# Decoder layer with 32 experts on one core: the experts' gather reads normalised rows, router, conversion and fill order rewritten

## The chip, the cores and the metric

One Trainium2 chip, one core of it. The metric is the device time of one launch in microseconds (us); of the kernel before three timed runs and one profiled execution are shown.

## What is computed

One inference step of one decoder layer (width 1024) for 256 prompt tokens and 8 sample tokens that share all weights:

```
y    = x @ w_in -> short convolution and dilated attention (12 heads)
x    = LN1(alpha * x + mixed @ w_out)
x    = LN2(alpha * x + memory_attention(x))          4 heads over 256 memory rows
g    = softmax of the 4 largest of (x @ w_router + b_router), 32 experts
y_e  = swiglu(x_e @ w_gate_up[e] + b_gate_up[e]) @ w_down[e] + b_down[e]
x    = LN3(alpha * x + sum over the chosen experts of g_e * y_e)
```

An expert's weights are 12 MB in float32 (8 MB gate and up, 4 MB down), 384 MB for all 32; everything else that is read is below 100 MB.

## The kernel before

Everything is written by hand as one stream of instructions for each engine, with semaphores between them. SP issues nearly all loads. A table of loads (`STREAM`) runs through a ring of 12 slots of 1 MB; a slot is loaded again when `reader_done` says that its reader is through.

**Projection and heads.** TensorE multiplies x by w_in in split float32 (`win_half`, L1641); after the second half `small_turns` (L1580 to L1588) makes the bias table and turns the small parameters (convolution weights, gains and shifts of the two norms) into columns; VectorE copies them out (L1015 to L1019) before it goes on with the low parts of w_in (L991). Then comes a pipeline over steps 0 to 13 for the 12 attention heads. In step s TensorE does `scores(s)` (L1689, L1690), `probs_turned(s - 1)` (transposes, L1697) and `values(s - 2)` (L1706 to L1708); VectorE does `head_max(s)`, in the steps `KEYS_AT = (1, 2, 4, 5, 6, 7, 8, 10)` also the key products and sums of one sample sequence (L1096, L1088), and then `head_norm(s)` (L1135), for which `probs_turned(s)` of the next step waits. In step 0 VectorE does the samples' own scores between the two. The table `FILL` puts 8 half products of the memory keys and values (`dense_half`, 8 matmuls of 128x512 each, L1608) behind the work of certain steps: `{1: 0, 2: 1, 4: 2, 5: 3, 7: 4, 8: 5, 10: 6, 11: 7}`.

**Second norm.** The output product of memory attention is the last `dense_half("wmo", 3)`, four tiles, between which TensorE does single small products of the samples' norm (`sample_means` L1809, `sample_squares` L1814); VectorE adds each tile to the residual (L1212) and computes the samples' norm (L1276 to L1292). `layer_norm(1)`: x is kept as columns (`xT`); TensorE turns it to rows in PSUM (L1822), VectorE takes the statistics, ScalarE writes the normalised rows `xh` (L892), TensorE turns them back (L1829, L1836), and ScalarE and VectorE apply gain and shift chunk by chunk (L896, L1249).

**Router.** Logits of all tokens in one product with w_router as the stationary side (L1935), bias (L1388), transposes of the logits (L1948), and of the finished x back to rows (L1942); VectorE finds the 4 largest (L1398 to L1413), TensorE counts (L1960, L1963), VectorE makes positions and the 0/1 matrix `Sel` (L1445), and ScalarE, VectorE and GpSimd cut the rows of x into three bfloat16 parts `x3` (L937, L1421, L941, L775; samples L1472, L1473). Then `gather` multiplies the parts with `Sel` (L1972, samples L1974), ScalarE copies the result to `xTe` (L952 or L962), VectorE makes the gates (L1477 to L1480), `SelG` (L1455), scales x by alpha (L1484) and copies the turned gates (L1488), and releases TensorE's expert loop.

**Experts.** Loop over 16 pairs of experts: `gate_up` (L2001) of both with the scatter of the pair before between its chunks (L2050), `down` (L2034), the turned activations (L2021), the next `gather`. 16 slots of 1 MB hold the experts' weights; SP fills them in units of two (L626, L622) as TensorE is done with each. After the last pair `sum_turned` (L2071) puts x as rows into PSUM, L2110 adds the last scattered results, and `last_layer_norm` (L1221, L1301, L1307) ends the kernel.

## Time and profile before

| what | value |
|---|---|
| median of 3 timed runs | 1330.09 us (1328.61 to 1330.22) |
| the profiled execution | 1329.79 us, its span 1328.0 us |
| TensorE busy, weight loads | 1228.7 us (93%), 580.6 us |
| VectorE, ScalarE, GpSimd busy | 375.4, 202.5, 39.0 us |
| moved by DMA | 485.08 MB, mean 365 GB/s |
| GB/s, slices 13 to 39 of 40 | 401, then 425 to 432 |
| GB/s, slice 12 | 135 |
| mean granted TensorE clock | 0.981 |

A slice is 33.2 us. Busy shares of engines are means over stages with different limits; a trace row gives the start, how long the group took, the engine, the line, what it writes and reads with shapes, how many records it has (a float32 matmul leaves two, a transpose or a bfloat16 matmul one), and in brackets how long the engine sat idle before it and what ended that.

### The profile page before, as it was taken

The page shows a single profiled execution, that of the slowest core. Times are in us where ns is not written, and L with a number is a line of the kernel's source. Part 1 is how long each engine was busy: PE and PEld are TensorE (multiplying, and loading weights), DVE is VectorE, ACT ScalarE, POOL GpSimd, SP SyncE. Part 2 cuts the span into 40 slices and gives each one's busy share as a digit, 9 for nine tenths or more (in the row PEclk, how much of TensorE's full clock was granted, in tenths as well). Part 3 has the DMA queues.
Part 4 walks back from the last instruction along what each step waited for, and adds up shares of the span by engine and source line. Part 5 has one row for each costly group of instructions (what it writes and reads, how often), then busy time and mean ns, then how long its engine had stood idle before and what let it go on. Part 6 is the DMA issues. An engine that isn't in the chain of part 4 may idle for free.

```text
span 1328.0 us, 16323 instructions
## 1 busy us (share of the span) xinstructions
PE 1228.7 (93%) x6536; PEld 580.6 (44%) x6536; DVE 375.4 (28%) x921; ACT 202.5 (15%) x334; POOL 39.0 (3%) x62
## 2 busy tenths in 40 slices
PE   7998999989879999999999998989899898989986
PEld 6994446675643343433433233333333233333323
DVE  3645532471353022121221302122020202212123
ACT  4443131122120110100101010010101011010001
POOL 2201000000010000000000000000000000000001
PEclk8998899999879999999999999999999999999998
DMA  9984767388939999999999999999999999999993
GB/s 324 246 273 164 215 214 268 107 328 331 365 135 401 426 426 428 426 430 427 427 427 427 428 428 429 426 427 428 427 426 432 426 426 427 427 427 427 428 425 128
DMA packets 62628, 485.08 MB, mean 365 GB/s; under 512 B 6176, under 2 KB 6516, under 8 KB 34336
## 3 DMA queue, kind: packets, MB, share of 16 engines
q1 hardware_dynamic: 58720, 469.46, 87.0%
q0 software_dynamic: 3872, 15.12, 3.5%
q8 instruction: 25, 0.41, 0.1%
q14 instruction: 11, 0.09, 0.0%
HBM read 479.40 MB, written 5.17 MB: 365 GB/s over the span
## 4 chain that ended last, share of the span: by engine, by line
PE 60%; DMA 33%; DVE 4%; ACT 1%; SPq 1%; issue 1%; DVEq 0%; ACTq 0%
PE ps L2001 25%; DMA ring<-in_w_gate_up_dram 15%; DMA late<-in_w_gate_up_dram 13%; PE ps L1608 10%; PE ps L1641 5%; PE ps L2050 5%; PE ps L2034 5%; DMA ring<-in_w_down_dram 3%; DMA ring<-in_cache_mem_v_dram 1%; PE ps L1972 1%; PE ps L1775 1%; PE ps L2058 1%; DVE arena L1221 1%; DMA ring<-in_w_in_dram 1%; PE ps L1793 1%
## 5 line engine op out<-in xcount | busy, mean ns | idle before, releaser
L2001 PE MATMUL ps<-ring,arena 128*64 128x512 f32 x1536 | 359.8, 600 | 14.9 <-DMA ring<-in_w_gate_up_dram 14.9
L1510 DVE TENSOR_TENSOR arena<-arena,ps 128x264 f32<-128x264 f32 x128 | 55.2, 431 | 574.5 <-PE ps L2050 574.5
L2001 PEld LDWEIGHTS ps<-ring,arena 128*64 128x64 f32 x1536 | 99.0, 136 | 201.3 <-issue 160.7
L2034 PE MATMUL ps<-ring,arena 128*64 128x512 f32 x768 | 171.3, 596 | 14.9 <-DMA ring<-in_w_down_dram 14.9
L2034 PEld LDWEIGHTS ps<-ring,arena 128*64 128x64 f32 x768 | 53.8, 137 | 119.7 <-issue 105.8
L957 ACT ACTIVATE arena<-arena 128x512 f32<-128x512 f32 x32 | 20.2, 632 | 471.2 <-DVE arena L1493 471.2
L2050 PE MATMUL ps<-arena 128*128 128x264 f32 x256 | 91.2, 438 | 0.0
L2001 PE MATMUL ps<-late,arena 128*64 128x512 f32 x384 | 90.0, 596 | 0.0
L1608 PE MATMUL ps<-arena,ring 128*128 128x256 f32 x384 | 87.0, 381 | 1.4 <-ACT arena L896 0.7
L2050 PEld LDWEIGHTS ps<-arena 128*128 128x128 f32 x256 | 38.1, 188 | 103.8 <-issue 103.8
L1641 PE MATMUL ps<-x_split,w_split 128*128 128x264 f32 x384 | 74.5, 295 | 7.3 <-DVE arena L1001 5.1
L1608 PEld LDWEIGHTS ps<-arena,ring 128*128 128x128 f32 x384 | 71.1, 189 | 14.4 <-issue 3.1
L1641 PEld LDWEIGHTS ps<-x_split,w_split 128*128 128x128 f32 x384 | 62.4, 197 | 7.9 <-DVE x_split L997 5.1
L1972 PE MATMUL ps<-arena 128*128 128x128 bf16 x768 | 54.9, 223 | 8.2 <-DVE arena L1473 8.2
L1608 PE MATMUL ps<-ring,arena 128*128 128x512 f32 x128 | 61.0, 632 | 0.0
L1641 PE MATMUL ps<-x_split,ring_split 128*128 128x264 f32 x192 | 56.2, 293 | 0.0
L1972 PEld LDWEIGHTS ps<-arena 128*128 128x128 bf16 x768 | 51.9, 100 | 8.4 <-issue 8.3
L2001 PE MATMUL ps<-arena 96*64 96x512 bf16 (+1 forms) x256 | 50.7, 495 | 4.0 <-DMA late<-in_w_gate_up_dram 3.1
L1493 DVE TENSOR_SCALAR arena<-ps 128x512 f32<-128x512 f32 x32 | 22.2, 693 | 109.9 <-PE ps L2001 109.4
L959 ACT COPY arena<-ps 128x512 f32<-128x512 f32 x32 | 18.8, 587 | 219.7 <-PE ps L2021 219.7
L2034 PE MATMUL ps<-late,arena 128*64 128x512 f32 x192 | 44.2, 595 | 6.2 <-DMA late<-in_w_down_dram 6.2
L2001 PEld LDWEIGHTS ps<-late,arena 128*64 128x64 f32 x384 | 25.8, 136 | 45.2 <-issue 42.2
(301 smaller groups left out, 983.2 us busy)
## 6 DMA issues: line engine op xcount, KB each, us to landing
ring<-in_w_gate_up_dram SPq DMA_DIRECT2D x96, 2048.0 KB, 33.8
ring<-in_w_down_dram SPq DMA_DIRECT2D x48, 2048.0 KB, 34.3
late<-in_w_gate_up_dram SPq DMA_DIRECT2D x16, 2048.0 KB, 33.8
arena<-in_w_gate_up_dram SPq DMA_DIRECT2D x16, 1024.0 KB, 31.5
late<-in_w_gate_up_dram SPq DMA_DIRECT2D x16, 1024.0 KB, 34.2
late<-in_w_down_dram SPq DMA_DIRECT2D x8, 2048.0 KB, 35.3
ring<-in_w_in_dram SPq DMA_DIRECT2D x12, 1024.0 KB, 16.9
ring<-in_cache_mem_k_dram SPq DMA_DIRECT2D x8, 1024.0 KB, 6.1
```

The source lines that it names most:

```text
L957: nc.scalar.activation(sg_, g2, ACT.Sigmoid, scale=1.702).then_inc(e_sig, 1)
L959: nc.scalar.copy(actT, ps[:, 2, :].rearrange("p (q n) -> p q n", q=4)).then_inc(e_at_out, 1)
L1221: nc.vector.bn_stats(stats[0:n, t, 6 * j:6 * j + 6], ps[0:n, bank + j, :]).then_inc(dve_own, 1)
L1493: nc.vector.tensor_scalar(g2, ps[:, b, :], 7.0, None, ALU.min).then_inc(e_g2, 1)
L1510: nc.vector.tensor_tensor(xT[:, c, :], xT[:, c, :], ps[:, 2 + c % 2, 0:T], ALU.add).then_inc(e_y_out, 1)
L1608: ins = mm(out(n), lhs(w, k, kk), rhs(w, k, kk), start=(kk == 0), stop=(kk == 7))
L1641: ins = mm(ps[:, n % 4, 0:T], w[:, cols], x[kk], start=(kk == 0 and m == 0), stop=(kk == 7 and m == 2))
L1775: ins = mm(out, w, v, start=(t == 0), stop=(t == terms[-1]))
L1972: mm(out, x3[:, t, k, P * c:P * c + P], Sel[:, t].rearrange("p a s -> p (a s)"), start=(t == 0 and k == 0), stop=False)
L2001: ins = mm(ps[64 * j:64 * j + 64, 6 * a + gu, :], x, w[:, D * gu + 512 * j:D * gu + 512 * j + 512], start=(c < 0), stop=(c == 7), skip_gro ...
L2034: ins = mm(ps[64 * j:64 * j + 64, 4 + half, :], x, w[:, kk, 512 * half:512 * half + 512], start=(m == 0), stop=(m == 7), skip_group_check= ...
L2050: mm(ps[:, 2 + c % 2, 0:T], yb[:, half, P * (c % 4):P * (c % 4) + P], SelT[:, half, :], start=True, stop=True).then_inc(e_y, 1)
```

## The change

1. `FILL` becomes `{0: 0, 1: 1, 3: 2, 5: 3, 7: 4, 8: 5, 10: 6, 11: 7}`; `KEYS_AT` stays.
2. `small_turns` also turns gain and shift of the second norm into columns in the order in which the gather delivers channels (8 more matmuls), with one more copy on VectorE.
3. The three bfloat16 parts are cut from the normalised rows `xh2`, before gain and shift: rows 0 to 127 by four instructions on GpSimd, rows 128 to 255 by three conversions on ScalarE, between which TensorE subtracts with `minus` (minus the identity) in PSUM. Gain and shift are applied behind the gather: channels 0 to 3 by four instructions on ScalarE, 4 to 7 by four on VectorE, with a semaphore each, and TensorE waits for the second only at chunk 4.
4. The samples' rows are taken as float32, turned in `sample_rows` inside `dense_half("wmo", 3)` behind its third tile (`sample_squares` moves up one tile), and gathered by a float32 matmul over 8 rows instead of a bfloat16 one over 72.
5. Logits are made per chunk with x as the stationary side (`logits_of`), between the transposes of the second norm, so that they come out as rows; those of the samples earlier (`sample_logits`, with 6 matmuls that only keep TensorE at work).
6. Memsets go from VectorE to GpSimd, before the norm. On VectorE the gates now stand behind `x_scaled(2)`.
7. In the last pair `sum_turned` stands inside `gate_up` and `down`, and the last norm's statistics wait for each half of a tile.

```diff
-FILL = {1: 0, 2: 1, 4: 2, 5: 3, 7: 4, 8: 5, 10: 6, 11: 7}
+FILL = {0: 0, 1: 1, 3: 2, 5: 3, 7: 4, 8: 5, 10: 6, 11: 7}
...
+            for tl in (lgt, posm):
+                nc.gpsimd.memset(tl, 0.0).then_inc(s_low, 1)
+            pool.wait_ge(s_sc, H + MH)
+            nc.gpsimd.memset(yb, 0.0).then_inc(s_yz, 1)
+            pool.wait_ge(s_yz, 1)
+            pool.dma_start(yb[0:NX], b_down[0].rearrange("e (h n) -> e h n", h=2)).then_inc(s_first, 16)
             pool.wait_ge(s_dn, 56)
             pool.dma_start(g3[:, 0, :], ln3_g.broadcast_to((P, D))).then_inc(s_g3, 16)
             pool.dma_start(g3[:, 1, :], ln3_b.broadcast_to((P, D))).then_inc(s_g3, 16)
-            pool.wait_ge(s_yz, 1)
-            pool.dma_start(yb[0:NX], b_down[0].rearrange("e (h n) -> e h n", h=2)).then_inc(s_first, 16)
-            for t in range(2):
-                pool.wait_ge(s_x2b, t + 1)
-                nc.gpsimd.tensor_tensor(x3[:, t, 2, :], rest[:, t, :], x3[:, t, 1, :], ALU.subtract).then_inc(s_x3, 1)
+            nc.gpsimd.memset(SelT, 0.0).then_inc(s_yz, 1)
+            hi0 = by_unit(x3[:, 0, 0, :])
+            pool.wait_ge(s_xh, 3)
+            nc.gpsimd.tensor_copy(hi0, every_second(xh2[:, 0, :])).then_inc(s_split, 1)
+            pool.wait_ge(s_split, 1)
+            nc.gpsimd.tensor_tensor(by_unit(rest), every_second(xh2[:, 0, :]), hi0, ALU.subtract).then_inc(s_split, 1)
+            pool.wait_ge(s_split, 2)
+            nc.gpsimd.tensor_copy(x3[:, 0, 1, :], rest).then_inc(s_split, 1)
+            pool.wait_ge(s_split, 3)
+            nc.gpsimd.tensor_tensor(x3[:, 0, 2, :], rest, x3[:, 0, 1, :], ALU.subtract).then_inc(s_split, 1)
...
+                if k == 1:
+                    act.wait_ge(s_srow, 1)
+                    act.wait_ge(s_xz, 1)
+                    nc.scalar.copy(by_unit(xs_rows[0:NS, :]), every_second(psf[0:NS, 3072:3072 + D])).then_inc(
+                        s_srow_out, 1)
+                rows_of = (xh, xh2)[k]
...
-            for t, (_, n) in enumerate(TCH):
-                act.wait_ge(s_x2, t + 1)
-                b = (4, 6, 2)[t]
-                if t == 0:
-                    act.wait_ge(s_xz, 1)
-                nc.scalar.copy(by_unit(x3[:, t, 0, :] if t < 2 else xs3[0:n, :]),
-                               every_second(psf[0:n, 512 * b:512 * b + D])).then_inc(s_x1, 1)
-            for t, (_, n) in enumerate(TCH):
-                act.wait_ge(s_xr, t + 1)
-                nc.scalar.copy(x3[:, t, 1, :] if t < 2 else mid_s[0:n, :],
-                               rest[:, t, :] if t < 2 else rest_s[0:n, :]).then_inc(s_x2b, 1)
-            act.wait_ge(s_rt_out, 3)
+            rest1 = psf[:, 512 * ROWB[1]:512 * ROWB[1] + D]
+            nc.scalar.copy(by_unit(x3[:, 1, 0, :]), every_second(xh2[:, 1, :])).then_inc(s_three, 1)
+            act.wait_ge(s_less, 1)
+            nc.scalar.copy(x3[:, 1, 1, :], rest1).then_inc(s_three, 1)
+            act.wait_ge(s_less, 2)
+            nc.scalar.copy(x3[:, 1, 2, :], rest1).then_inc(s_three, 1)
+            act.wait_ge(s_route, 2)
             nc.scalar.activation(rex, rex, ACT.Exp).then_inc(s_gex, 1)
+            def x_scaled(n):
+                act.wait_ge(e_gx, n)
+                for c in range(4):
+                    ins = nc.scalar.activation(xTe[:, c, :], ps[:, 6, P * c:P * c + P], ACT.Identity,
+                                               bias=gather_gb[:, 1, c:c + 1], scale=gather_gb[:, 0, c:c + 1])
+                ins.then_inc(e_gx_out, 1)
...
-                dve.wait_ge(s_ln, 2 * k + i + 1)
+                if k < 2:
+                    dve.wait_ge(s_ln, 2 * k + i + 1)
                 for j in range(2):
+                    if k == 2:
+                        dve.wait_ge(s_ln, 4 + 2 * i + j + 1)
...
+                if k == 1:
+                    dve.wait_ge(s_low, 5)
+                    dve.wait_ge(s_rts, 1)
+                    link(nc.vector.tensor_tensor(lgt[0:NS, 2, :], ps[0:NS, 7, 2 * NX:3 * NX], brow[0:NS, :], ALU.add))
+                    link(nc.vector.max(top8[:, 2, :], lgt[:, 2, :]))
...
-                link(nc.vector.tensor_tensor(x_s, x_s, tokens(sums_s[:, 0, :]), ALU.mult))
-                link(nc.vector.tensor_tensor(x_s, x_s, channels(gcol[k]), ALU.mult))
+                nc.vector.tensor_tensor(squares_s, x_s, tokens(sums_s[:, 0, :]), ALU.mult).then_inc(s_xhs, 1)
+                dve.wait_ge(s_xhs, k + 1)
+                link(nc.vector.tensor_tensor(x_s, squares_s, channels(gcol[k]), ALU.mult))
...
-            dve.wait_ge(s_kvst, 96)
-            for tl in (lgt, posm, gat, SelT, yb):
-                ins = nc.vector.memset(tl, 0.0)
-                if tl is not yb:
-                    own[0] += 1
-                    ins.then_inc(dve_own, 1)
-            ins.then_inc(s_yz, 1)
-            dve.wait_ge(dve_own, own[0])
             dve.wait_ge(s_rt, 1)
-            nc.vector.tensor_scalar(lgTs[0:NX, :], ps[0:NX, 0, 0:T], brc[0:NX, :], None, ALU.add).then_inc(
-                s_rt_out, 1)
-            dve.wait_ge(s_rt, 2)
-            own[0] += 2
-            nc.vector.tensor_copy(lgt[:, 0:2, :], ps[:, 1, 0:2 * NX].rearrange("p (t e) -> p t e", t=2)).then_inc(
-                dve_own, 1)
-            nc.vector.tensor_copy(lgt[0:NS, 2, :], ps[0:NS, 1, 2 * NX:3 * NX]).then_inc(dve_own, 1)
-            dve.wait_ge(dve_own, own[0])
-            for t in range(3):
+            link(nc.vector.tensor_tensor(lgt[:, 0:2, :], ps[:, 6, 0:2 * NX].rearrange("p (t e) -> p t e", t=2),
+                                         brow.unsqueeze(1).broadcast_to((P, 2, NX)), ALU.add))
+            for t in range(2):
...
+            def x_scaled(n):
+                dve.wait_ge(e_gx, n)
+                for c in range(4, DC):
+                    ins = nc.vector.tensor_scalar(xTe[:, c, :], ps[:, 7, P * (c - 4):P * (c - 4) + P],
+                                                  gather_gb[:, 0, c:c + 1], gather_gb[:, 1, c:c + 1], ALU.mult,
+                                                  ALU.add)
+                ins.then_inc(e_gx_odd, 1)
             select(0)
...
+            x_scaled(2)
...
+                every = par_rows[0:n_par, :].rearrange("p (q s) -> p s q", s=2)
+                for i in range(2):
+                    row = 6 + DC * (2 + i)
+                    to = ps[:, 6, 96 + DC * i:96 + DC * i + DC].rearrange("p (u s) -> p s u", s=2)
+                    for j in range(2):
+                        of_row = ident[0:n_par, row:row + DC].rearrange("p (u j) -> p j u", j=2)[:, j, :]
+                        for s in range(2):
+                            ins = mm(to[64 * j:64 * j + 64, s, :], every[:, s, :], of_row, start=True, stop=True)
+                ins.then_inc(s_bt, 1)
...
+            def sample_rows():
+                pe.wait_ge(s_xhs, 2)
+                for c in range(DC):
+                    ins = tp(psf[0:NS, 3072 + P * c:3072 + P * c + P], squares_s[:, c, :], ident)
+                ins.then_inc(s_srow, 1)
+            def sample_logits():
+                pe.wait_ge(s_xs, 2)
+                pe.wait_ge(s_srow_out, 1)
+                pe.wait_ge(s_late, 16)
+                for c in range(DC):
+                    ins = mm(ps[0:NS, 7, 2 * NX:3 * NX], x_s[:, c, :], wr[:, c, :], start=(c == 0), stop=(c == DC - 1),
+                             skip_group_check=True)
+                ins.then_inc(s_rts, 1)
+                stay_awake(6, ps[:, 6, 0:P])
+            def logits_of(c):
+                for t in range(2):
+                    ins = mm(ps[:, 6, NX * t:NX * t + NX], xT[:, c, P * t:P * t + P], wr[:, c, :], start=(c == 0 and t == 0),
+                             stop=(c == DC - 1), skip_group_check=True)
+                return ins
...
+                    if k == 1:
+                        logits_of(c - 4)
+                for c in range(4, DC):
+                    pe.wait_ge(s_lt_odd if c % 2 else s_lt_out, 4 * k + c // 2 + 1)
+                    if k == 1:
+                        ins = logits_of(c)
+                if k == 1:
+                    ins.then_inc(s_rt, 1)
...
-            dense_half("wmo", 3, out_columns, {0: lambda: sample_means(1), 2: lambda: sample_squares(1)})
-            layer_norm(1)
-            pe.wait_ge(s_xs, 2)
-            pe.wait_ge(s_late, 16)
-            for c in range(DC):
-                ins = mm(ps[0:NX, 0, 0:T], wr[:, c, :], xT[:, c, :], start=(c == 0), stop=(c == 7))
-            ins.then_inc(s_rt, 1)
-            def x2_rows(t):
-                (t0, n), b = TCH[t], (4, 6, 2)[t]
-                for c in range(DC):
-                    ins = tp(psf[0:n, 512 * b + P * c:512 * b + P * c + P], xT[:, c, t0:t0 + n], ident)
-                ins.then_inc(s_x2, 1)
-            x2_rows(0)
-            pe.wait_ge(s_rt_out, 1)
-            for t, (t0, n) in enumerate(TCH):
-                ins = tp(ps[0:n, 1, NX * t:NX * t + NX], lgTs[0:NX, t0:t0 + n], ident[0:NX, 0:NX])
-            ins.then_inc(s_rt, 1)
-            x2_rows(1)
-            x2_rows(2)
-            stay_awake(8, ps[:, 0, 384:512])
-            pe.wait_ge(s_rt_out, 2)
-            pe.wait_ge(s_low, 2)
+            dense_half("wmo", 3, out_columns, {0: lambda: sample_means(1), 1: lambda: sample_squares(1),
+                                               2: sample_rows})
+            layer_norm(1, sample_logits)
...
+            rest1 = [ps[:, ROWB[1] + j, :] for j in range(2)]
+            pe.wait_ge(s_low, 5)
+            for j in range(2):
+                rows = every_second(xh2[:, 1, :])[:, 2 * j:2 * j + 2]
+                mm(rest1[j], ident, rows, start=True, stop=False, skip_group_check=True)
+            pe.wait_ge(s_three, 1)
+            for j in range(2):
+                ins = mm(rest1[j], minus, x3[:, 1, 0, 512 * j:512 * j + 512], start=False, stop=True,
+                         skip_group_check=True)
+            ins.then_inc(s_less, 1)
...
-                    ins = mm(out, xs3[0:64 + NS, P * c:P * c + P], Sel[0:64 + NS, 2].rearrange("p a s -> p (a s)"),
+                    ins = mm(out, xs_rows[0:NS, P * c:P * c + P], SelS[0:NS].rearrange("p a s -> p (a s)"),
                              start=False, stop=True)
-                ins.then_inc(e_gx, 1)
-            pe.wait_ge(s_xr, 3)
-            pe.wait_ge(s_x3, 4)
+                    if c % 4 == 3:
+                        ins.then_inc(e_gx, 1)
...
+                    if last and a == 1 and c == 3:
+                        pe.wait_ge(e_st_out, 3 * it + 4)
+                        sum_turned(1, 1)
+                        pe.wait_ge(e_u2, 2 * it + 2)
+                        sum_turned(2, 0)
+                    if last and a == 1 and c == 4:
+                        sum_turned(2, 1)
...
-                if last:
-                    pe.wait_ge(e_st_out, 3 * it + 4)
-                    for t, half in ((2, 0), (2, 1), (1, 1), (0, 0), (0, 1)):
-                        sum_turned(t, half)
-                else:
+                if not last:
```

TensorE in the attention steps 0 to 2. Before (L1689 and L1690 are scores, L1697 the transposes, L1608 a fill):

```order
L1689 MATMUL ps<-arena 128x128
L1690 MATMUL ps<-arena 128x256
L1689 MATMUL ps<-arena 128x128
L1690 MATMUL ps<-arena 128x256
L1697 MATMUL ps<-arena,late 128x128 x3
L1608 MATMUL ps<-ring,arena 128x512 x8
L1689 MATMUL ps<-arena 128x128
L1690 MATMUL ps<-arena 128x256
L1697 MATMUL ps<-arena,late 128x128 x3
```

and with the change (the same instructions are L1721, L1722, L1729 and L1640):

```order
L1721 MATMUL ps<-arena 128x128
L1722 MATMUL ps<-arena 128x256
L1640 MATMUL ps<-ring,arena 128x512 x8
L1721 MATMUL ps<-arena 128x128
L1722 MATMUL ps<-arena 128x256
L1729 MATMUL ps<-arena,late 128x128 x3
L1640 MATMUL ps<-ring,arena 128x512 x8
L1721 MATMUL ps<-arena 128x128
L1722 MATMUL ps<-arena 128x256
L1729 MATMUL ps<-arena,late 128x128 x3
```

The first fill stands ahead of the first transposes, and step 2 no longer has one.

TensorE from the last half product (L1640) to the first transposes of the second norm (L1879), with the change (L1841 means, L1846 squares, L1852 `sample_rows`, L1861 `sample_logits`):

```order
L1640 MATMUL ps<-arena,ring 128x256 x4
L1841 MATMUL ps<-arena 128x8
L1640 MATMUL ps<-arena,ring 128x256 x4
L1846 MATMUL ps<-arena 128x8
L1640 MATMUL ps<-arena,ring 128x256 x4
L1852 MATMUL ps<-arena 8x128 x8
L1640 MATMUL ps<-arena,ring 128x256 x4
L1879 MATMUL ps<-arena 128x128 x16
L1861 MATMUL ps<-arena 8x32 x8
```

Before, tiles 2 and 3 were one row of x8, the squares (L1814) stood behind them, and nothing stood for L1852 and L1861.

VectorE from the selection to the last copy before the expert loop, with the change (L1452 and L1454 `Sel`, L1475 `x_scaled(2)`, L1491 to L1494 the gates, L1464 to L1468 `advance`, L1497 alpha, L1502 the turned gates):

```order
L1454 TENSOR_TENSOR arena<-arena,late 128x256
L1458 CAST arena<-arena 96x128
...
L1486 TENSOR_SCALAR nswi<-late 1x1 x4
L1475 TENSOR_SCALAR arena<-ps,arena 128x128 x4
L1491 TENSOR_TENSOR late<-late 128x96
...
L1494 TENSOR_TENSOR late<-late 128x96
...
L1497 TENSOR_SCALAR arena<-arena 128x2112
L1502 COPY arena<-ps 32x264 x2
```

Before, nothing of L1475 stood there, and two instructions for the samples' parts (L1472, L1473) stood in its place.

## Rows read from the trace of the kernel before

**Rows 1.** Chain that ended last, start us, us, what

```profile
306.14 16.86 DMA ring<-in_cache_mem_v_dram
...
410.72 2.27 PE ps L2001 x12
...
464.62 2.27 PE ps L2001 x12
...
1220.99 34.60 DMA ring<-in_w_gate_up_dram
```

**Rows 2.** Windows: busy us of PE, PEld, DVE, ACT, POOL; PEclk; DMA share; GB/s

```profile
384.00:386.00 2.00, 1.94 (x19) 1.97 (x20) 1.86 (x7) 0.00 (x0) 0.00 (x0) 0.50 0.00 0
```

**Rows 3.** Timeline of TensorE, projection: the small turns and what follows

```profile
30.45 0.61 PE L1582 MATMUL ps<-arena 33*128 33x12 f32 x4
...
33.83 0.39 PE L1641 MATMUL ps<-x_split,w_split 128*128 128x264 f32 x1 [2.19 <-DVE ring_split L991]
```

**Rows 4.** Timeline of TensorE in the attention steps

```profile
108.00 0.90 PE L1697 MATMUL ps<-arena,late 128*128 128x128 f32 x3 [3.39 <-DVE late L1135]
...
119.77 7.13 PE L1608 MATMUL ps<-ring,arena 128*128 128x512 f32 x16
...
130.50 0.55 PE L1697 MATMUL ps<-arena,late 128*128 128x128 f32 x3 [0.62 <-DVE late L1135]
...
154.01 0.90 PE L1697 MATMUL ps<-arena,late 128*128 128x128 f32 x3 [2.93 <-DVE late L1135]
...
156.31 9.18 PE L1608 MATMUL ps<-ring,arena 128*128 128x512 f32 x16
```

**Rows 5.** Timeline, last half product before the second norm

```profile
351.63 1.97 PE L1608 MATMUL ps<-arena,ring 128*128 128x256 f32 x8
...
352.70 0.23 DVE L1290 TENSOR_TENSOR arena<-arena 128x64 f32<-128x64 f32 x1
...
354.12 1.97 PE L1822 MATMUL ps<-arena 128*128 128x128 f32 x16 [0.52 <-DVE arena L1212]
```

**Rows 6.** Timeline from the norm to the first expert's release

```profile
361.99 1.97 PE L1836 MATMUL ps<-arena 128*128 128x128 f32 x8
...
372.03 0.38 DVE L1398 MAX8 late<-late 128x8 f32<-128x32 f32 x3
...
374.16 0.26 DVE L1413 TENSOR_TENSOR late<-late 128x96 bf16<-128x96 f32 x1
...
383.99 0.26 DVE L1477 TENSOR_TENSOR late<-late 128x96 f32<-128x96 f32 x1
...
384.06 0.80 PE L1972 MATMUL ps<-arena 128*128 128x128 bf16 x6 [8.19 <-DVE arena L1473]
...
385.62 1.25 DVE L1484 TENSOR_SCALAR arena<-arena 128x2112 f32<-128x2112 f32 x1
...
390.13 0.76 DVE L1488 COPY arena<-ps 32x264 f32<-32x264 f32 x2 [3.26 <-PE ps L1984]
...
390.96 0.62 PE L2001 MATMUL ps<-arena 96*64 96x512 bf16 x4 [0.86 <-ACT arena L952]
...
395.05 0.33 SPq L626 DMA_DIRECT2D late<-in_w_down_dram  x1
```

**Rows 7.** Timeline of VectorE and GpSimd side by side

```profile
379.67 1.92 DVE L1465 TENSOR_SCALAR late<-arena,late 1x4 f32<-1x4 f32 x1
...
379.58 2.00 POOL L775 TENSOR_TENSOR arena<-arena 128x1024 bf16<-128x1024 f32 x1 [0.44 <-ACT arena L941]
```

**Rows 8.** Timeline, the end of the kernel

```profile
1294.85 3.65 PE L2034 MATMUL ps<-ring,arena 128*64 128x512 f32 x16 [1.16 <-DMA ring<-in_w_down_dram]
...
1299.11 5.68 PE L2071 MATMUL ps<-arena 128*8 128x128 f32 x48
...
1304.73 7.09 PE L2034 MATMUL ps<-ring,arena 128*64 128x512 f32 x32
...
1314.76 1.30 DVE L1221 BATCH_NORM_STATS2 arena<-ps 128x6 f32<-128x512 f32 x2 [2.21 <-PE ps L2110]
```

194 lines of the change are left out of this document (105 added, 89 removed).

## The prediction

> **What bounds the kernel now.** I read the chain that ended last first, then windows, then the timeline around each edit. Up to the expert loop the chain is mostly TensorE's own matmuls. It leaves them once for long: memory values that SP issued at 306.14 land at 323.0 [rows 1]. That issue came when VectorE had freed the ring, and VectorE followed TensorE, so the wait moves along with whatever stands ahead of it. I let every us of the prologue count.
>
> In the loop the first two pairs follow each other at 464.62 - 410.72 = 53.9 us [rows 1], TensorE's pace while slots are full. Later the chain is nothing but DMA: 24 loads of 1 MiB (25.17 MB together) at the 427 GB/s of the profile's slices take 58.9 us a pair. The 5 us between make the loop DMA's. Its end is therefore the time at which SP's first issue follows a released slot, 395.05 [rows 6], plus a constant; before that issue the queue lies dry (0 GB/s in 384 to 386, [rows 2]). So **three things count: TensorE's time up to 395.05, nothing inside the loop, and what follows the last landing** [rows 8].
>
> The sum is made against the profiled execution, 1329.79 us, which is 0.3 under the median of the runs; I take them as one. A measurement of this kernel tells about 0.2% (2.7 us) from no change.
>
> **Small turns.** Eight float32 matmuls more, two records each; four records of twelve columns take 0.61 us at first [rows 3], and I take 0.12 us a record: 8 x 2 x 0.12 = 1.9 us. TensorE waits for VectorE already there, 2.19 us [rows 3], and VectorE's copies wait for the turns, so the added time lengthens that wait, and a fifth copy of 0.15 us comes on top. If some lies beside the start of a load it is less: **+1.7**, between 0 and +2.1.
>
> **Fill order.** In steps without a fill TensorE waits for `head_norm`. Before, these waits are 3.39 us (step 0, VectorE also at the samples' scores), 0.62 (step 3, no key products), 2.93 (step 6, key products), and 0.62 again in step 9, which I take from step 3's row: 7.6 us [rows 4]. Now step 0 has a fill of 7.13 us, longer than its wait, and that wait goes. Steps 2, 4, 6 and 9 have none; the first three hold key products, so each should wait 2.93, and step 9 0.62: 9.4 us. Net +1.9. What the old 3.39 hid was VectorE's first step; the 7.13 us cover it.
> Then the clock. Behind each of the two long waits the transposes take 0.90 us instead of 0.55 and the fill 9.18 instead of 7.13 [rows 4], so one fall costs 0.35 + 2.05 = 2.4 us. Behind three such waits it is three falls against two: +2.4. Steps 2 and 4 follow each other closely, so one may fall less than the next: with two falls the part is +1.9, with none 1.9 - 4.8 = -2.9. I take three, since both long waits of before fell and neither short one did: **+4.3**, between -2.9 and +4.3, with +2 more if what follows a fall is longer than the fill.
>
> **Sample rows in the last half product.** TensorE now wants the samples' normalised values behind tile 2, which ends where tile 3's row begins, 351.63. The squares come one tile earlier, but on VectorE the variance still stands behind tile 2's residual (the order of the part on the change), so the values are ready where L1290 ends, 352.93 [rows 5]. TensorE, which ran through, idles 1.3 us with the signal's way, some 1.4, then turns eight chunks, half of L1822's 16 in 1.97 us: 1.0 [rows 5]. **+2.4** before the norm, between +1.0 (values in time) and +3.
>
> **Second norm and router,** counted from T0, the norm's first transpose (354.12). Before, they reach the first `gate_up` at T0 + 36.8 and the gather at T0 + 29.9 [rows 6]; between them stand logits for all tokens, three turns to rows and three rounds of conversion. Now, step by step: turning back ends at T0 + 9.8 [rows 6] plus about 1.2 for the logits put between, plus 0.7 for the last two chunks' gain and shift, plus the last logits: T0 + 12.7. VectorE adds the bias (0.3) and takes two maxima (0.3), then the unchanged chain from the maxima's end to L1413's, 374.42 - 372.41 = 2.0: T0 + 15.4. Counts on TensorE 1.3, the second subtraction 0.5, ScalarE's third conversion of 1024 columns some 1.0 (VectorE's L1484 needs 1.25 for 2112, [rows 6]): T0 + 18. GpSimd starts at T0 + 5 and needs four instructions of 2.0 us each [rows 7], T0 + 13, so it has 5 us in hand. Gather: with the clock full it is half of before's 5.7 us, 3.3 with waits, plus 1.4 for a float32 sample product of two records in place of one in 8 chunks; at half clock it takes 0.5 to 3 more. T0 + 22.7. Then, in VectorE's row, four scalings of 128 columns, 0.35 each between L1290's 0.23 for 64 [rows 5] and L1488's 0.38 for 264 (1.4), gates and `advance` 385.62 - 383.99 = 1.6, alpha 1.25, copies 0.76 [rows 6]: T0 + 27.7, **9.1 us earlier** than 36.8. Here an old cover is gone: before, gates and alpha stood beside a gather of 5.7 us; now TensorE idles some 5 us ahead of `gate_up`. In this profile an idle stretch of 8.19 us [rows 6] left the granted clock at 0.50 [rows 2]. `gate_up` to the release is 4.1 us [rows 6] at full clock; I take +2.4 for the half one, as in the fill, +1.0 for VectorE instructions held up by GpSimd's and +0.5 for the gather. **-5.2**, between -9 and -2.
>
> That VectorE can be held up by GpSimd shows once in the trace: L1465, one partition of four elements, takes 1.92 us and ends with GpSimd's L775 [rows 7]. The Trainium skill's "SBUF — State Buffer", Who interferes with whom, says that a VectorE instruction with two SBUF inputs, or in a two-port mode, and a GpSimd one that reads SBUF shut each other out for the whole instruction. The row agrees; the rule speaks against part 3 of the change, and is behind the second rival.
>
> **Samples and scaling in the loop.** The 1.4 us of float32 sample products make TensorE's pace 55.3 us a pair, still 3.6 under DMA's 58.9; ScalarE's four scalings and VectorE's four stand beside matmuls. Nothing. If DMA did not bind, 14 pairs of 1.4 would be 20 us.
>
> **The end.** The last expert's `down` needs the last two units of 2 MiB. Before, the sums (5.68 us) stand right ahead of it. A unit lands every 4.9 us (2.1 MB at 427 GB/s), and TensorE needs 3.65 us for it [rows 8]. The last then lands near 1294.85 + 2 x 4.9 = 1304.65, and its product ends at 1308.3, where `down` of before ends at 1304.73 + 7.09 = 1311.8 because the sums stood ahead. Only one sum of 0.95 stays behind. -3.1, and the last norm's statistics start on half a tile, which takes about half of 1.30 off: -0.6. **-3.7**, between -4.5 and -1.
>
> **Sum:** 1.7 + 4.3 + 2.4 - 5.2 - 3.7 = -0.5 us: 1329.3.
>
> **Rivals.**
> **1, faster: the clock holds.** TensorE does transposes and values between the waits of steps 2 and 4, and both old falls stood behind something special (step 0 and step 6 with long gaps since the last fill). For it: the 0.62 waits cost nothing. With one fall at most in the heads (-2.9 + 2.4 = -0.5 in place of +4.3) the time is 1324.5; with `gate_up` at full clock too, -2.4 more, 1322.1. Against: a wait of 2.93 fell once already. I take 1325. Chance 0.32.
> **2, slower: GpSimd's conversions come late.** They read every second element, which no row shows on GpSimd, and stand against VectorE's two-input instructions of norm and router. Up to T0 + 18 this is free. From there each us counts. If the two strided ones take twice 2.0, the chain ends at T0 + 5 + 12 = T0 + 17; two or three instructions of VectorE's chain held for 1.9 each [rows 7] then push the selection, hence counts and TensorE's second subtraction, to about T0 + 22: +4, and the gather at half clock another 1.5. 1329.3 + 5.5 = 1334.8. By the rule of that page of the Trainium skill this is what would happen wherever a router instruction meets one of GpSimd's; the row bears it out for one. Chance 0.24.
> **3, the end gains nothing or the loop turns TensorE's.** The sums may stand where TensorE has no pause, and DMA's 58.9 may hide the rest: 3.5 us less gained, 1332.8. Chance 0.08, of which half counts as slower.
> My forecast keeps 0.36.
>
> **Chances.** Faster by over 0.2% (under 1327.4): rival 1 and a little of the forecast's lower side, 0.38. Within: 0.37. Slower (over 1332.7): rival 2 and parts of the forecast and rival 3, 0.25. The likeliest case's own range is 1327 to 1332.5. The range for 8 in 10 must take in both rivals: from 1321.5 (rival 1 whole) to 1336 (rival 2 and a further us of its locks).
>
> **What would show it.** Small turns: the wait ahead of the products that follow them 4 us, not 2.2. Fill: three waits of 2.9 in steps 2, 4, 6, each with transposes of 0.90 behind, none in step 0. Sample rows: TensorE idle 1.6 us ahead of them, released by VectorE. Router: gather starts at T0 + 18, released by ScalarE and not by GpSimd; `gate_up` at T0 + 27.7; PEclk 0.50 there. GpSimd: four instructions of 2 us; VectorE ones stretched to about 2 beside them. End: no sums between the last `down`s, last landing minus first release unchanged. I am wrong if the loop's pace per pair is not 58.9, if the landings move by other than the first release, or if the gather waits for GpSimd.

## The result, and the profile after

The changed kernel is slower: 1344.49 us median of four runs (1343.38 to 1345.7) against 1330.15, ratio 1.0113 with a 95% interval of 1.010 to 1.0125. I had forecast 1329.3 and a range up to 1336. Its profiled execution took 1343.38 us, its span 1341.6.

| us | before | after | difference | forecast |
|---|---|---|---|---|
| first transpose of the second norm (T0) | 354.12 | 363.12 | +9.0 | +8.4 |
| T0 to the gather's start | 29.94 | 24.06 | -5.9 | -11.9 |
| gather's start to first `gate_up` | 6.90 | 15.92 | +9.0 | +2.8 |
| first `gate_up` to SP's first issue | 4.09 | 6.65 | +2.6 | +2.4 |
| that issue to the end of the span | 932.95 | 931.85 | -1.1 | -3.7 |

(The forecast also held 1.5 us for locks and a half-clock gather in rows two and three together.) Up to T0 the forecast stands. From T0 to the release it was 10.9 us off (+5.7 where I had -5.2), and 2.6 more at the end.

From the page of the changed kernel: the clock and GB/s of 40 slices, the shares of the chain that ended last, and groups of instructions (busy us, mean ns, idle before).

```profile
PEclk8999799999959999999999999999999999999999
...
GB/s 324 246 267 176 192 201 264 114 299 367 307 163 285 427 426 427 427 428 427 426 428 427 429 427 428 427 427 428 425 429 428 427 427 427 427 425 429 427 426 147
...
PE 91%; DVE 4%; DMA 2%; ACT 1%; SPq 1%; issue 1%; DVEq 0%; ACTq 0%
...
L2031 PE MATMUL ps<-arena 128*128 128x128 bf16 x768 | 67.5, 225 | 1.1 <-ACT arena L959 1.1
...
L2033 PE MATMUL ps<-arena 8*128 8x128 f32 x256 | 64.2, 331 | 0.0
...
L2062 PE MATMUL ps<-ring,arena 128*64 128x512 f32 x1536 | 358.7, 600 | 0.0
```

Slice 12 has a clock of five tenths, and the chain is 91% TensorE where it was a third DMA. TensorE waits for nothing before its expert products now (0.0 us idle in 1536 records): the loop is no longer DMA's. The 256 records of the samples' float32 product take 331 ns each, half as long again as the 225 ns of a bfloat16 record.

**Attention steps,** timeline of TensorE in the changed kernel, steps 2 to 6:

```profile
126.69 0.55 PE L1729 MATMUL ps<-arena,late 128*128 128x128 f32 x3 [2.93 <-DVE late L1158]
...
127.96 8.83 PE L1640 MATMUL ps<-ring,arena 128*128 128x512 f32 x16
...
142.70 0.90 PE L1729 MATMUL ps<-arena,late 128*128 128x128 f32 x3 [2.93 <-DVE late L1158]
...
159.94 0.90 PE L1729 MATMUL ps<-arena,late 128*128 128x128 f32 x3 [2.93 <-DVE late L1158]
```

Three waits of 2.93 us as forecast. Behind the second and the third the transposes take 0.90 us at once; behind the first the clock fell only within the fill that follows (8.83 us instead of 7.13). Cf. [rows 4].

**From the half product to the first release,** all engines in the changed kernel:

```profile
359.83 1.04 PE L1852 MATMUL ps<-arena 128*8 128x128 f32 x8 [1.33 <-DVE arena L1321]
...
363.12 1.97 PE L1879 MATMUL ps<-arena 128*128 128x128 f32 x16 [0.52 <-DVE arena L1235]
...
368.40 0.86 DVE L1260 SCALAR_TENSOR_TENSOR arena<-arena 128x1 f32<-128x1 f32 x1
...
370.56 1.00 PE L1886 MATMUL ps<-arena 128*128 128x128 f32 x4 [1.77 <-ACT arena L914]
...
375.57 4.32 PE L1869 MATMUL ps<-arena 128*128 128x32 f32 x20
...
379.70 3.76 PE L2000 MATMUL ps<-arena 128*128 128x512 f32 x4
...
382.22 0.26 DVE L1433 TENSOR_TENSOR late<-late 128x96 bf16<-128x96 f32 x1
...
385.42 0.11 PEld L2021 LDWEIGHTS ps<-arena,late 128*128 128x128 bf16 x2 [0.65 <-ACT arena L957]
...
387.18 0.50 PE L2031 MATMUL ps<-arena 128*128 128x128 bf16 x6 [1.15 <-ACT arena L959]
...
397.78 0.50 PEld L2033 LDWEIGHTS ps<-arena 8*128 8x128 f32 x2 [0.20 <-issue]
...
398.61 1.37 DVE L1475 TENSOR_SCALAR arena<-ps,arena 128x128 f32<-128x128 f32 x4 [11.65 <-PE ps L2033]
...
403.10 1.06 PE L2062 MATMUL ps<-arena 96*64 96x512 bf16 x4 [1.39 <-DVEq L1529]
...
409.75 0.33 SPq L633 DMA_DIRECT2D late<-in_w_down_dram  x1
```

Windows of the same stretch (busy us of PE, PEld, DVE, ACT, POOL; PEclk; DMA share; GB/s):

```profile
374.00:376.00 2.00, 2.00 (x12) 2.00 (x11) 0.20 (x2) 1.35 (x2) 0.65 (x1) 0.50 1.08 461
...
386.00:388.00 2.00, 0.85 (x9) 0.71 (x8) 0.85 (x8) 1.92 (x2) 0.00 (x0) 0.95 0.01 4
...
390.00:392.00 2.00, 2.00 (x14) 1.38 (x12) 0.00 (x0) 0.00 (x0) 0.00 (x0) 0.50 0.00 0
...
404.00:406.00 2.00, 2.00 (x8) 0.66 (x6) 0.00 (x0) 0.00 (x0) 0.00 (x0) 0.50 0.00 0
```

To be seen here: the sample rows wait 1.33 us, as I had it. VectorE's L1260 takes 0.86 us beside GpSimd's first instruction (0.16 for the other tile), and TensorE idles 1.77 us between the halves of the turn back. Behind that the clock falls: it is 0.50 from about 370.7 to 384.4, through the logits and the product with the identity (L2000, 3.76 us), then full, and 0.50 again from about 387.8 to 408.3, through nearly the whole gather (387.18 to 398.57) and the first `gate_up`. The counts stand behind L2000 in TensorE's row, though VectorE has the selection at 382.48.

The kernel before had half clock in this stretch too. A window of its norm:

```profile
362.00:364.00 2.00, 1.96 (x8) 1.56 (x8) 1.13 (x4) 1.39 (x3) 0.00 (x0) 0.50 0.96 363
```

Its clock was 0.50 from about 358.4 to 368.7, and from about 378.9 to 389.2 ahead of and in its gather: 20.5 us together between T0 and the release, against 34.1 in the changed kernel. Half clock was not new there; there is more of it now, and more of it lies under work that everything waits for.

**A later pair's gather.** Timeline of TensorE in the changed kernel:

```profile
736.78 0.50 PE L2031 MATMUL ps<-arena 128*128 128x128 bf16 x6
...
737.22 0.48 PE L2033 MATMUL ps<-arena 8*128 8x128 f32 x2
...
737.63 0.51 PE L2031 MATMUL ps<-arena 128*128 128x128 bf16 x6
```

and in the kernel before:

```profile
710.26 0.50 PE L1972 MATMUL ps<-arena 128*128 128x128 bf16 x6
...
710.60 0.22 PE L1974 MATMUL ps<-arena 72*128 72x128 bf16 x1
...
710.66 0.50 PE L1972 MATMUL ps<-arena 128*128 128x128 bf16 x6
```

At full clock a chunk starts 0.85 us after the one ahead of it, and 0.40 before. Eight chunks make 3.6 us a pair: the pairs follow each other at 488.20 - 430.71 = 57.5 us instead of 53.9 [rows 1].

**The end.** Timeline of TensorE in the changed kernel, and below it two windows:

```profile
1310.90 1.86 PEld L2141 LDWEIGHTS ps<-arena 128*128 128x128 f32 x16 [0.81 <-issue]
...
1312.88 0.20 PEld L2102 LDWEIGHTS ps<-ring,arena 128*64 128x64 f32 x4
...
1318.98 0.20 PEld L2102 LDWEIGHTS ps<-ring,arena 128*64 128x64 f32 x4
```

```profile
1316.00:1318.00 2.00, 1.32 (x9) 0.67 (x5) 0.00 (x0) 0.59 (x1) 0.00 (x0) 1.00 0.48 205
...
1318.00:1320.00 2.00, 2.00 (x14) 1.31 (x16) 0.00 (x0) 0.00 (x0) 0.00 (x0) 1.00 0.04 16
```

The last landing is near 1317, but the last `down` runs until 1326.07, 9 us behind it. Before, a like window (1302 to 1304) had 123 GB/s, so the last landing was near 1302.6, and `down` ended at 1311.8, 9.2 us behind; but then 5.68 us of sums stood right ahead of it [rows 8]. From the first release to the last landing it was 907.5 us before and 907.2 now: the landings moved with the release, as I had said, and DMA kept its rate. What is new is that TensorE itself is late. The sums do stand ahead of the last `down`, but TensorE has no wait for DMA left for them to fill.

### The profile page after: what moved, and what is told of

Same layout as the page of the kernel before. It is cut to its first block, busy times and chain, and to the rows that moved or that the text cites. A ratio compares the mean times of both kernels' runs of the same rounds, so it can differ in the third digit from the quotient of the medians.

```text
span 1341.6 us, 16810 instructions
## 1 busy us (share of the span) xinstructions
PE 1290.4 (96%) x6697; PEld 620.7 (46%) x6697; DVE 389.8 (29%) x1002; ACT 208.2 (16%) x380; POOL 43.1 (3%) x68
## 4 chain that ended last, share of the span: by engine, by line
PE 91%; DVE 4%; DMA 2%; ACT 1%; SPq 1%; issue 1%; DVEq 0%; ACTq 0%
PE ps L2062 36%; PE ps L2102 17%; PE ps L1640 10%; PE ps L2120 6%; PE ps L1673 5%; PE ps L2031 4%; PE ps L2033 4%; PE ps L2089 2%; DMA ring<-in_cache_mem_v_dram 1%; PE ps L1807 1%; PE ps L2128 1%; DMA ring<-in_w_in_dram 1%; PE ps L1825 1%; DVE arena L1247 1%; PE ps L1869 0%
## 5 line engine op out<-in xcount | busy, mean ns | idle before, releaser
L2062 PE MATMUL ps<-late,arena 128*64 128x512 f32 x384 | 92.1, 608 | 0.0
L1640 PE MATMUL ps<-arena,ring 128*128 128x256 f32 x384 | 87.1, 381 | 1.6 <-DVE arena L1280 0.9
L1640 PEld LDWEIGHTS ps<-arena,ring 128*128 128x128 f32 x384 | 71.0, 189 | 14.6 <-issue 3.1
L1475 DVE TENSOR_SCALAR arena<-ps,arena 128x128 f32<-128x128 f32 x64 | 21.9, 405 | 184.8 <-PE ps L2033 184.8
L2031 PE MATMUL ps<-arena 128*128 128x128 bf16 x768 | 67.5, 225 | 1.1 <-ACT arena L959 1.1
L2033 PE MATMUL ps<-arena 8*128 8x128 f32 x256 | 64.2, 331 | 0.0
L1640 PE MATMUL ps<-ring,arena 128*128 128x512 f32 x128 | 62.4, 644 | 0.0
L2031 PEld LDWEIGHTS ps<-arena 128*128 128x128 bf16 x768 | 46.6, 100 | 16.1 <-issue 3.2
```

Of the source, the lines that this page charges most:

```text
L1475: ins = nc.vector.tensor_scalar(xTe[:, c, :], ps[:, 7, P * (c - 4):P * (c - 4) + P], gather_gb[:, 0, c:c + 1], gather_gb[:, 1, c:c + 1], A ...
L1640: ins = mm(out(n), lhs(w, k, kk), rhs(w, k, kk), start=(kk == 0), stop=(kk == 7))
L2031: mm(out, x3[:, t, k, P * c:P * c + P], Sel[:, t].rearrange("p a s -> p (a s)"), start=(t == 0 and k == 0), stop=False)
L2033: ins = mm(out, xs_rows[0:NS, P * c:P * c + P], SelS[0:NS].rearrange("p a s -> p (a s)"), start=False, stop=True)
L2062: ins = mm(ps[64 * j:64 * j + 64, 6 * a + gu, :], x, w[:, D * gu + 512 * j:D * gu + 512 * j + 512], start=(c < 0), stop=(c == 7), skip_gro ...
```

## Experiments

Each kernel was timed beside the kernel before on the same chip (its median 1329.7 to 1329.9 in the three sets). "Release" is SP's first issue for a slot that the expert loop freed; it was 395.05 before and is 409.75 in the changed kernel.

**1. Fill order alone, undone in the changed kernel and done in the old one.**

```diff
-FILL = {0: 0, 1: 1, 3: 2, 5: 3, 7: 4, 8: 5, 10: 6, 11: 7}
+FILL = {1: 0, 2: 1, 4: 2, 5: 3, 7: 4, 8: 5, 10: 6, 11: 7}
```

> The changed kernel with the fill order of before. TensorE reaches the second norm at 363.12 us in the changed kernel and at 354.12 before; 4.75 us of these 9.0 arise in the attention steps, and about 1 more in the memory attention, where a wait of 1.95 us left the clock at half. Theory 'fill order' expects the norm's first transpose about 4.8 to 5.8 us earlier (357.3 to 358.3), and as TensorE never waits in the expert loop of the changed kernel, the whole of it at the end: 1338.7 to 1339.7. A rival, 'the memory values' transfer covers it' (TensorE waits until 329.6 for them anyway), expects less than 3 us.

> The kernel before with the new fill order alone. Theory 'fill order': three waits of 2.93 us and three clock falls in the attention steps in place of 3.39, 0.62, 2.93 and two falls cost 4.75 us there, as in the changed kernel; the loop of this kernel is DMA's, so its end follows the first release: 1334.5 to 1335.5, against 1329.7 to 1330.1. The rival (the memory values' transfer hides part of it) expects 1331.5 to 1333.

Measured: 1339.14 us (1336.95 to 1339.89) with it undone, 5.4 less; T0 at 358.12. Done alone in the old kernel: 1334.13 (ratio 1.0029, 1.0018 to 1.0041), 4.3 more; T0 at 358.97, 4.85 later. The order of the fills costs 5.4 us in one kernel and 4.3 in the other (0.4 under the range I had given there), so little of it is covered by anything.

**2. GpSimd later.**

```diff
-            pool.wait_ge(s_xh, 3)
+            pool.wait_ge(s_xh, 4)
```

> The changed kernel, but GpSimd starts its four conversions only when both tiles of normalised rows are written (a wait for 4 in place of 3). In the changed kernel VectorE's L1260 takes 0.86 us beside GpSimd's first conversion (0.16 without), TensorE then idles 1.77 us between the two halves of the turn back, and its clock is at half from about 370.7 to 384. Theory 'lock' expects L1260 at 0.16 us, an idle time of about 1.05 as before, a clock that stays full in the norm as it does before, and so logits 3 to 4 us earlier and the gather about 3 us earlier: 1341 to 1342. Theory 'the clock falls anyway' (the chunks' turns and logits are too thin for it) expects 0.7 us only: 1343.8. GpSimd ends at about T0 + 14, under the gather's T0 + 24, in both.

VectorE's scaling, the halves of the turn back and the last logits in that kernel:

```profile
369.13 0.16 DVE L1260 SCALAR_TENSOR_TENSOR arena<-arena 128x1 f32<-128x1 f32 x1
...
370.59 0.66 PE L1886 MATMUL ps<-arena 128*128 128x128 f32 x4 [1.06 <-ACT arena L914]
...
375.58 4.31 PE L1869 MATMUL ps<-arena 128*128 128x32 f32 x20
```

In this profile the hold-up is gone (0.16 us, 1.06 idle) and the clock falls all the same: the logits take 4.31 us as before the edit, the gather starts 23.3 us behind T0 instead of 24.1, and the release, at 409.81, 45.95 us behind T0 instead of 46.63. GpSimd's part is 0.7 us here. But the median was 1341.36 (1340.61 to 1344.1), 3.1 us under the changed kernel's and where the theory "lock" had put it. The profile is of the slowest run (1344.1 us, mean granted clock 0.973); the other three took 1340.61 to 1341.53 at 0.975, and the four runs of the changed kernel had 0.971 to 0.973. So in those three TensorE was probably at half clock for less time, which no trace shows: GpSimd's part is between 0.7 and some 3 us and stays open. The expectation's premise that the clock was full in this place in the kernel before was wrong (window above).

**3. Keeping TensorE at work.** `stay_awake(n)` are n products of the identity with itself:

```diff
-                stay_awake(6, ps[:, 6, 0:P])
+                stay_awake(9, ps[:, 6, 0:P])
...
                 for t in range(2):
+                    if k == 1 and t == 1:
+                        stay_awake(5, ps[:, 6, 0:P])
...
+            stay_awake(2, ps[:, 6, 0:P])
             pe.wait_ge(s_three, 2)
...
+            stay_awake(4, ps[:, 6, 0:P])
             pe.wait_ge(s_split, 4)
...
             gather()
+            stay_awake(10, ps[:, 0, 384:512])
...
+            stay_awake(5, ps[:, 0, 384:512])
             pe.wait_ge(s_nsw, 4)
```

> The changed kernel with more matmuls that only keep TensorE at work: 3 more ahead of the turn back, 5 between its halves, 2 and 4 around the second subtraction, 10 after the gather, 5 after the turned gates (each some 0.26 us at full clock, so about as long as the waits they stand in). Theory 'clock' says that of the 12.1 us by which gate_up starts later and of the 2.6 us to the first release after it most of what lies behind T0 is the half clock: chunks and logits 4 us, the product with the identity 1.9, gather 5.7, gate_up 2.6. It expects the first release 9 to 13 us earlier than 409.75 and a time of 1331 to 1335.5. Theory 'added work' says that instructions, not the clock, make it late, and expects under 4 us less (above 1340.5). If the fillers themselves come late or hold the path it is slower than the changed kernel.

> The changed kernel with fillers only in the second norm (3 and 5 more), none ahead of the gather or behind it. It tells whether the fall in the norm is the cause of all later ones. The clock should be full until about T0 + 20, and the gather start at about T0 + 19 instead of 24.1, as in the run with all fillers. Theory 'each wait makes its own fall': TensorE waits 0.6 and 1.2 us ahead of the gather, which stays at half clock for the most part (11 us instead of 6.7), and waits 4 us behind it: first release 4.5 to 6 us earlier than 409.75 and 1338.5 to 1340. Theory 'one fall': 1332 to 1334.

With all of them (windows as above; T0 is 363.54 here):

```profile
374.00:376.00 2.00, 2.00 (x21) 2.00 (x19) 0.55 (x1) 1.27 (x2) 1.08 (x1) 1.00 0.96 403
...
386.00:388.00 2.00, 2.00 (x18) 1.43 (x19) 0.00 (x0) 1.98 (x4) 0.00 (x0) 1.00 0.00 0
...
394.00:396.00 2.00, 2.00 (x14) 0.76 (x12) 0.00 (x0) 0.00 (x0) 0.00 (x0) 1.00 0.04 8
```

The clock is 1.00 in every window up to the loop. The gather starts at T0 + 18.5, the number of my prediction, `gate_up` at T0 + 30.1, the release at 397.74, 12.0 us earlier, and the time is 1331.19 (1328.24 to 1332.5): 13.3 us less for more instructions, and level with the kernel before (ratio 1.0008, 0.9998 to 1.0017). The theory "clock" held, "added work" fell.

With the norm's fillers alone:

```profile
374.00:378.00 4.00, 3.65 (x21) 1.75 (x20) 2.51 (x12) 1.01 (x1) 0.00 (x0) 1.00 1.03 432
...
386.00:390.00 4.00, 4.00 (x23) 2.82 (x21) 0.00 (x0) 2.56 (x5) 0.00 (x0) 0.50 0.00 0
```

Full in the norm, at half in the gather: it starts at T0 + 18.1 but lasts until 391.6, and the release is at 402.15. 1336.88 us (1332.96 to 1337.7), 7.6 less and 1.6 under what I had expected; T0 happened to lie 1.4 us earlier in this profile, so 6.2 of the release's 7.6 us lie behind T0. The fall in the norm and the one ahead of the gather are two, and filling the waits of the norm did not hold the clock in the gather.

**4. The samples' float32 product,** left out, and then made of bfloat16 parts again (hi, mid, low in partitions 0, 32, 64 of one 72-row product; ScalarE and VectorE cut them in pauses).

```diff
-                    ins = mm(out, xs_rows[0:NS, P * c:P * c + P], SelS[0:NS].rearrange("p a s -> p (a s)"),
+                    ins = mm(out, xs3[0:64 + NS, P * c:P * c + P], SelS[0:64 + NS].rearrange("p a s -> p (a s)"),
                              start=False, stop=True)
```

> The changed kernel without the float32 product of the samples' rows in the gather; the kernel leaves the samples' part of the experts' input out. In the changed kernel a pair of experts takes TensorE 57.5 us instead of 53.9, and the last down ends 9 us behind the last landing, which is TensorE's doing. Theory 'float32 product' says that the eight products cost 0.45 us each at full clock: it expects 53.5 us a pair while slots are full, TensorE waiting for DMA again late in the loop, a first gather shorter by 8 x 0.65 = 5 us, and at the end 5 us from the first release plus 5 from the end bound by DMA again (last down 3.7 to 4 us behind the last landing): 1334 to 1336. The rival 'the loop is DMA's and only the prologue counts' (my prediction's view) expects 5 us less, 1339.5.

> The changed kernel with nothing but the samples' rows put back as three bfloat16 parts over 72 rows. Theory 'float32 product': the first gather, at half clock, loses 8 x 0.73 = 5.8 us, the first release comes near 404, a pair takes TensorE 53.9 us and the loop is DMA's again, so the end is before's plus (404 - 395.05) less the 3.7 us of the last part: 1335 to 1336. The rival 'only the prologue counts' expects 5.8 less than the changed kernel: 1338.7.

Left out: 1333.69 us (1331.91 to 1335.35), release 402.70, TensorE waiting 15.4 us for gate and up weights again (expected: 1334 to 1336). With bfloat16 parts: 1334.89 (1332.85 to 1335.59), 9.6 us less than the changed kernel; release 401.58, pairs at 476.46 - 422.55 = 53.9 us, 14.2 us of waits for DMA, a first gather from 385.66 to 390.6, 4.9 us instead of 11.4. (T0 happened to lie 1.5 us earlier in that profile.) The product costs twice: once in the first gather, and once by making the loop TensorE's.

**5. Together.** Old fill order and all fillers; then the bfloat16 parts as well; and, without these parts, the samples' turn behind the last tile.

```diff
-                                               2: sample_rows})
+                                               3: sample_rows})
```

> The changed kernel with the matmuls that keep the clock up (as in the run before, which gave 1331.2 and its first release at 397.7 us) and the old fill order. The two lie in different places of the program, so they should add: first release near 392.5, TensorE still at 57.5 us a pair and the bound to the end: 1326 to 1326.5. If the loop had turned DMA's again it would be no less than 1324; if the fill order's 5 us were covered by something, 1330.

> As the kernel with old fill order and fillers, and the samples' rows again as three bfloat16 parts in one product over 72 rows, the parts cut in pauses of ScalarE and VectorE. Theory 'float32 product': a pair takes TensorE 53.9 us, DMA binds the loop again, the first gather is 3.6 us shorter, so the first release comes near 389 us, 6 us earlier than before the change, and 3.7 us are gained at the end as I had predicted for it: 1319.5 to 1321.5. The rival 'the loop was DMA's anyway' expects only the 3.6 us: 1322.5 to 1323. If the extra VectorE and ScalarE work holds the norm up, 1 to 2 us more.

> As the kernel with old fill order and fillers, but the turn of the samples' rows stands behind the last tile of the half product instead of the third. In the changed kernel TensorE idles 1.33 us ahead of it and spends 1.04 us on it; behind the last tile it would stand in a wait of 0.52 us: the norm should start 1.9 us earlier (0.5 us of the 2.4 left), and the end moves with it, 1.9 us under the kernel with old fill order and fillers: 1324 to 1324.5. A rival, that ScalarE's copy of the rows then holds up the norm's square roots, expects no gain.

Old fill order and fillers: 1326.92 us (1325.45 to 1328.99, 0.4 over the expected range), release 391.80, TensorE still without a wait in the loop. With bfloat16 parts: 1320.25 (1319.21 to 1321.19; ratio 0.993, 0.9914 to 0.9947), release 388.17. Here the group of expert products reads

```profile
L2088 PE MATMUL ps<-ring,arena 128*64 128x512 f32 x1536 | 360.0, 600 | 14.0 <-DMA ring<-in_w_gate_up_dram 14.0
```

so the loop is DMA's, and 3.6 us of earlier release brought 6.7 us. The samples' turn moved: 1325.22 (1323.56 to 1326.32), 1.7 less than without, where 1.9 was expected; T0 at 355.60 instead of 357.75, 2.15 us earlier, of which 1.15 arrive at the release.

**6. The end alone.** In the fastest of these the sums go back between the `down`s:

```diff
-                    if last and a == 1 and c == 3:
-                        pe.wait_ge(e_st_out, 3 * it + 4)
-                        sum_turned(1, 1)
-                        pe.wait_ge(e_u2, 2 * it + 2)
-                        sum_turned(2, 0)
-                    if last and a == 1 and c == 4:
-                        sum_turned(2, 1)
...
-                down(r, 2 * j, sum_first if last else None)
+                down(r, 2 * j)
...
+                if last:
+                    pe.wait_ge(e_st_out, 3 * it + 4)
+                    for t, half in ((2, 0), (2, 1), (1, 1), (0, 0), (0, 1)):
+                        sum_turned(t, half)
```

> The kernel with old fill order, fillers and bfloat16 samples (1320.3 us), with the sums of the last pair put back to where they stood before, between the two downs; the statistics' wait per half stays. In that kernel DMA binds the loop, so the sums moved into TensorE's waits should be worth what I had predicted for them, 3.1 us: 1323 to 1323.7. In the rival, where TensorE has no pause at the end, it makes no difference: 1320.3.

Timeline with the sums put back, and below it without:

```profile
1292.98 5.68 PE L2160 MATMUL ps<-arena 128*8 128x128 f32 x48
...
1298.59 7.09 PE L2121 MATMUL ps<-ring,arena 128*64 128x512 f32 x32
```

```profile
1294.09 1.16 PE L2167 MATMUL ps<-arena 128*128 128x128 f32 x8 [0.68 <-ACT arena L986]
...
1295.17 7.09 PE L2128 MATMUL ps<-ring,arena 128*64 128x512 f32 x32
```

1323.51 us (1322.63 to 1324.16), 3.3 more. From the release to the end of the span it is 932.4 us instead of 929.7; the other 0.7 lay ahead of the release in these two profiles. So the moved sums are worth 2.7 to 3.3 us where DMA binds the loop; I had said 3.1.

**7. The waits of the attention steps filled too.**

```diff
                 ins.then_inc(s_bt, 1)
+                stay_awake(8, ps[:, 7, 384:512])
...
                 if step < H:
                     scores(step)
+                if step in {1: 12, 7: 10}:
+                    if step >= 3:
+                        pe.wait_ge(s_av_out, step - 2)
+                    stay_awake({1: 12, 7: 10}[step], ps[:, 7, 384:512])
```

> The kernel with old fill order, fillers and bfloat16 samples (1320.3 us), with 12 and 10 more fillers in the two long waits of the attention steps (steps 1 and 7) and 8 in the wait behind the small turns. Each of the two falls in the attention steps costs 2.4 us and the one behind the small turns some 2 us, by the rows of before; the loop is DMA's, so its end follows the first release: 1313.5 to 1315. If fillers only move a fall to a later place, less than 3 us of it shows.

The fillers (L1645), transposes and fill of step 7 in that kernel, and a window behind the small turns:

```profile
148.91 2.50 PE L1645 MATMUL ps<-arena 128*128 128x128 f32 x20 [0.46 <-ACT arena L872]
...
151.38 0.55 PE L1749 MATMUL ps<-arena,late 128*128 128x128 f32 x3
...
152.66 7.13 PE L1660 MATMUL ps<-ring,arena 128*128 128x512 f32 x16
```

```profile
34.00:36.00 2.00, 2.00 (x11) 2.00 (x10) 2.00 (x3) 0.00 (x0) 0.00 (x0) 0.50 1.05 388
```

1314.17 us (1312.86 to 1314.35; ratio 0.9877, 0.9861 to 0.9894), T0 5.6 us and the release (382.55) 5.6 us earlier than in the kernel it is made from. Transposes and fill are at full clock. Behind the small turns the fillers held no clock: TensorE was busy from 31.83 on and the clock still went to 0.50. This version beats both kernels. How much of that the change and how much the fillers alone would give is not shown: no run puts fillers into the kernel before, which was at half clock for 20.5 us of the stretch behind T0 as well.

## Why the prediction was wrong

By its own steps:

- **What bounds the kernel.** The end is the release plus a constant within each group of versions, but the constant is not one. It was 932.95 us before, 929.5 to 930.1 in the four versions with the moved sums and without the float32 product, where DMA binds, and 931.9 to 932.8 in the seven with that product, where TensorE does.
- **Small turns,** +1.7: right in sign, 0.95 measured at the end of the projection. The 16 records took 0.67 us, not 1.9; the rest is the clock, which came back at 39.6 us instead of 37.6. In five later profiles with the same small turns it came back between 37.5 and 38.2, so this rest changes from run to run; two of these five with the new fill order have T0 at 361.60 and 361.71. That the sum up to T0 agrees to 0.6 us is in part luck.
- **Fill order,** +4.3: right, 4.75 us by the end of the attention steps (203.25 against 197.55, less the 0.95), three waits and three falls.
- **Sample rows,** +2.4: right, 1.33 us of waiting and 1.04 of turning. In the memory attention one more fall (L1984 of the changed kernel takes 2.81 us instead of 1.89, behind a wait of 1.95 us that the kernel before had as well) was not in my sum; the memory values' transfer took 1.1 us of it back. T0 +9.0 for my +8.4.
- **Second norm and router, -5.2: this failed,** it measures +5.7 (release minus T0: 46.63 for 40.93). Three terms of it: (a) "Gather: with the clock full it is half of before's ... plus 1.4". The 1.4 is 0.18 us a chunk. Among bfloat16 products the float32 one costs 0.45 us more than the bfloat16 one at full clock and 0.73 at half, 3.6 and 5.8 us in a gather. (b) I looked for half clock only ahead of `gate_up`, where I found it rightly (6.65 us for 4.09), and treated logits and gather as at full clock with an allowance of 0.5. With the clock held, the gather starts at T0 + 18.5, where I had T0 + 18; in the changed kernel at T0 + 24.1. (c) L2000, the float32 product with the identity, was missing: 3.76 us at half clock ahead of the counts, hidden behind VectorE's chain only at full clock. The fillers give back 12.0 us of the release, the bfloat16 parts at full clock 3.6.
- **Samples and scaling in the loop, nothing: this failed by the same price.** 53.9 + 1.4 = 55.3 should have read 57.5. That is still under DMA's 58.9, but the comparison of paces was the wrong test. TensorE has 16 pairs to do, 16 x 57.5 = 920 us; DMA starts with 16 slots full and needed 907 us from the release to the last landing. With 16 x 55.3 = 885 TensorE would, by this estimate, have kept up.
- **The end, -3.7:** right in size where DMA binds (2.7 to 3.3 measured for the sums). The way to it was not right: the landing that I had put at 1304.65 was near 1302.6, and the last `down` ends not 3.65 us behind the landing but some 6.7 in the kernel with old fill order, fillers and bfloat16 parts (landing near 1295.5 by its windows, end at 1302.26). Two errors of like size cancel, which is luck. The statistics' halves gave 0.65: from the end of the last `down` to the end of the span it is 15.5 us instead of 16.2. In the changed kernel only 1.1 us are left, because TensorE ends late. My third rival named this ("the loop turns TensorE's") with 0.08, and priced it 3.5 us; it cost 2.6.
- **Rival 1,** the clock holds: no, it fell three times in the attention steps and more often behind.
- **Rival 2,** GpSimd late: no. GpSimd's four instructions took 1.10, 2.14, 1.03 and 2.00 us and ended at T0 + 11.5. One VectorE instruction was held for 0.7 us. The Trainium skill's "SBUF — State Buffer", Who interferes with whom, has the rule for it: a VectorE instruction with two SBUF inputs contends with a GpSimd one that reads SBUF. The trace agrees (0.86 beside GpSimd, 0.16 without). As a cause of the lost time it is worth 0.7 us by the trace and at most some 3 by the times.

Of float32 the Trainium skill's "FP8 and Floating Point Precision", TensorE Precision Notes, says that a true float32 product is four passes through the array. Among products of its own kind the trace agrees: twenty records of ten fillers take 2.50 us (L1645 above), 0.25 us a product of 128 columns, about four times the 0.057 of a bfloat16 one (seven in 0.40 us). The samples' product between bfloat16 ones takes 0.41. The weights' load is not the reason by its length, for it is as long in the fillers (191 ns a record) as there (189). Whether it is the eight rows or the neighbours of another type no run separates.
